# Forgetting attention: the gate bias of the scores spread over the partitions by one transfer per head and added in PSUM by VectorE, in place of a matmul by TensorE

## The reference, cut to what matters

```
c = cumsum(log_sigmoid(f_logit), axis=1)            # (heads, tokens), one value per head and token
s = q @ k.T / sqrt(dh)
s = s + c[query] - c[key]
s = where(key <= query, s, -inf)
p = softmax(s);  o = p @ v
```

## Time and profile before

| what | value |
|---|---|
| median of 3 runs | 1056.45 us (1056.3 to 1057.19) |
| the profiled execution, its own time | 1057.25 us |
| its span (first to last instruction) | 1055.4 us |
| PE busy | 1047.5 us (99%) |
| DVE busy | 750.2 us (71%) |
| ACT busy | 593.8 us (56%) |
| mean granted TensorE clock | 0.998 of full speed |

### The profile page before, as it was taken

The page is one execution under the profiler, slowest core; times in us unless marked ns, Lnnn a source line. Parts: engine busy times, 40 slices in busy tenths (PEclk is TensorE's granted clock), DMA queues, the critical chain, the costliest instruction groups (busy, mean ns, idle before and its releaser), DMA issues.

```text
span 1055.4 us, 12979 instructions
## 1 busy us (share of the span) xinstructions
PE 1047.5 (99%) x4971; PEld 875.6 (83%) x4971; DVE 750.2 (71%) x898; ACT 593.8 (56%) x794; POOL 75.5 (7%) x59
## 2 busy tenths in 40 slices
PE   9999999999999999999999999999999999999997
PEld 7888888888888888888888888888889988888886
DVE  5768778885786676467986878868778666767642
ACT  6573776764484645448754545554366657565531
POOL 1200000000000000000454600000000000000000
PEclk9999999999999999999999999999999999999999
DMA  9944999986488777555547855979975345777741
GB/s 355 399 131 172 302 298 291 303 259 197 176 276 248 241 232 233 183 207 192 160 160 226 241 172 169 285 243 334 318 246 186 118 166 208 238 244 230 247 161 40
DMA packets 94765, 239.68 MB, mean 227 GB/s; under 512 B 14785, under 2 KB 39537, under 8 KB 94577
## 3 DMA queue, kind: packets, MB, share of 16 engines
q1 hardware_dynamic: 91136, 227.32, 66.9%
q0 software_dynamic: 3136, 11.23, 2.9%
q10 hardware_dynamic: 432, 0.33, 0.1%
HBM read 218.38 MB, written 20.45 MB: 226 GB/s over the span
## 4 chain that ended last, share of the span: by engine, by line
PE 90%; DVE 4%; ACT 2%; DMA 2%; issue 2%; SPq 0%; DVEq 0%; ACTq 0%
PE ps L810 21%; PE ps L808 21%; PE ps L809 21%; PE ps L845 5%; PE ps L847 5%; PE ps L846 5%; DVE rest L1936 1%; PE ps L942 1%; PE ps L1132 1%; ACT high L1363 1%; PE ps L1248 1%; PE ps L1250 1%; PE ps L1249 1%; DMA mk_blocked<-mem_turned 1%; DMA mem_turned<-mk_blocked 1%
## 5 line engine op out<-in xcount | busy, mean ns | idle before, releaser
L1936 DVE TENSOR_TENSOR rest<-raw,high 128x2048 fp32r<-128x2048 f32 x129 | 294.3, 2297 | 78.2 <-ACT high L1363 77.7
L808 PE MATMUL ps<-high,xt_high 128*128 128x512 f32 x824 | 324.6, 394 | 0.2 <-DVE rest L1936 0.2
L810 PE MATMUL ps<-high,xt_rest 128*128 128x512 f32 x824 | 320.9, 389 | 0.0
L809 PE MATMUL ps<-rest,xt_high 128*128 128x512 f32 x824 | 320.8, 389 | 0.0
L1363 ACT ACTIVATE high<-raw 128x2048 fp32r<-128x2048 f32 x129 | 244.3, 1910 | 67.8 <-DMA raw<-in_units_dram 67.7
L810 PEld LDWEIGHTS ps<-high,xt_rest 128*128 128x128 f32 x824 | 154.7, 188 | 32.3
L808 PEld LDWEIGHTS ps<-high,xt_high 128*128 128x128 f32 x824 | 154.8, 188 | 31.8 <-DVE rest L1936 0.6
L809 PEld LDWEIGHTS ps<-rest,xt_high 128*128 128x128 f32 x824 | 154.8, 188 | 31.1
L1941 DVE SCALAR_TENSOR_TENSOR rest<-raw,wgain,high 128x512 fp32r<-128x512 f32 x176 | 119.0, 746 | 35.4 <-ACT high L1367 35.4
L1367 ACT ACTIVATE high<-raw,wgain 128x512 fp32r<-128x512 f32 x176 | 110.9, 716 | 9.1 <-DMA raw<-in_units_dram 9.0
L1623 ACT ACTIVATE act<-ps,recips 128x256 f32<-128x256 f32 x44 | 18.4, 470 | 85.0 <-PE ps L810 85.0
(11 more groups left out here) (365 smaller groups left out, 1450.7 us busy)
## 6 DMA issues: line engine op xcount, KB each, us to landing
raw<-in_units_dram SPq DMA_DIRECT2D x350, 512.0 KB, 4.7
gv_turned<-gv_blocked SPq DMA_DIRECT2D x11, 512.0 KB, 5.6
gv_t<-gv_turned SPq DMA_DIRECT2D x44, 128.0 KB, 4.1
turned<-blocked SPq DMA_DIRECT2D x22, 256.0 KB, 5.3
hid_t<-turned SPq DMA_DIRECT2D x88, 64.0 KB, 4.1
raw<-in_units_dram SPq DMA_DIRECT2D x8, 256.0 KB, 5.2
fp_turned<-fpT SPq DMA_DIRECT2D x8, 192.0 KB, 2.7
fpT<-fp_turned SPq DMA_DIRECT2D x32, 48.0 KB, 3.6
```

The costliest lines, as they stand in the source:

```text
L808: pe.matmul(out, sh, wh, start=first, stop=False)
L809: pe.matmul(out, sh, wr, start=False, stop=False)
L810: mm = pe.matmul(out, sr, wh, start=False, stop=last)
L1936: vec.tensor_tensor(rest[:, slot, c], raw[:, slot, c], high[:, slot, c].bitcast(F32), ALU.subtract).then_inc(unit_rest, 1)
```

## The change

The bias matmul of each head is taken out of PE's work, with the matrix `identr`, the cleared buffer, the rounded copy and the remainder. The eight rows of `fcum` go to a DRAM tensor once. Per head, one transfer reads that head's row from DRAM to all 128 partitions (128 x 256 float32 numbers, 128 KB written), into one of two buffers. DVE adds it to the scores in PSUM with two instructions (128 and 256 columns) before it takes the maxima. The mask matmul now opens the accumulation. SP gets the new function `spread_biases`, called last in each load: the store on load 13 of `win2`, the transfer of head h on load 31 + h.

```diff
-        fbias = place("fbias", [P, P + S], F32R, area + 62 * KB)
+        fbias = place("fbias", [P, 2, S], F32, area + 62 * KB)
...
+        fcum_dram = nc.dram_tensor("fcum_rows", (HH, S), F32, kind="Internal").ap()
+        fcum_stored, fbias_landed = sem("fcum_stored"), [sem(f"fbias_landed{n}") for n in range(2)]
...
                 turn_probabilities(u)
+                spread_biases(u)
...
+            def spread_biases(u):
+                if u == UNIT["win2"] + 13:
+                    sync.wait_ge(sem("fcum_ready"), 1)
+                    sync.dma_start(fcum_dram, fcum[0:HH, :]).then_inc(fcum_stored, 16)
+                h = u - UNIT["win2"] - 31
+                if 0 <= h < HH:
+                    if h == 0:
+                        sync.wait_ge(fcum_stored, 16)
+                    if h >= 2:
+                        sync.wait_ge(sem("fox_max"), TT * (h - 1))
+                    sync.dma_start(fbias[:, h % 2, :], fcum_dram[h].partition_broadcast(P)).then_inc(fbias_landed[h % 2], 16)
...
-                    pe.matmul(out[:, 0:P + S], identr[:, n:n + 1].to_broadcast([P, P]), fbias[:, :], start=True, stop=False)
-                    pe.matmul(diagonal, identb[:, :], causal[:, :, :], start=False, stop=False)
+                    pe.matmul(diagonal, identb[:, :], causal[:, :, :], start=True, stop=False, skip_group_check=True)
...
-                        pe.wait_ge(sem("fcum_rest"), 2)
...
-                if u == 8:
-                    act.wait_ge(sem("fcum_ready"), 1)
-                    for c0, w in ((0, P), (P, S)):
-                        act.activation(fbias[0:FROWS, c0:c0 + w], fcum[:, 0:w], ACT.Copy).then_inc(sem("fcum_high"), 1)
...
                     elif what == "i":
+                        act.wait_ge(fcum_stored, 16)
...
-                    step(vec.memset(fbias[:, :].bitcast(F32), 0.0))
...
                         src = aux(("fs", n))
+                        vec.wait_ge(fbias_landed[n % 2], 16 * (n // 2 + 1))
+                        for c0, w in ((0, P), (P, S)):
+                            step(vec.tensor_tensor(src[:, c0:c0 + w], src[:, c0:c0 + w], fbias[:, n % 2, 0:w], ALU.add))
+                        settle()
...
-                if u == 8:
-                    vec.wait_ge(sem("fcum_high"), 2)
-                    r = slice(FROWS - HH, FROWS)
-                    for c0, w in ((0, P), (P, S)):
-                        vec.tensor_tensor(fbias[r, c0:c0 + w], fcum[r, 0:w], fbias[r, c0:c0 + w].bitcast(F32), ALU.subtract)\
-                            .then_inc(sem("fcum_rest"), 1)
```

More of the change, by code:

```diff
@@ L262, in build @@
             ("recips", [P, TT * len(NORMS)], F32), ("moments", [P, TT, 12], F32),
-            ("meanvar", [P, TT, 2], F32), ("identr", [P, HH], F32R), ("eps", [P, 2 + 2 * TT], F32), ("negmax", [P, HH, 2], F32),
+            ("meanvar", [P, TT, 2], F32), ("eps", [P, 2 + 2 * TT], F32), ("negmax", [P, HH, 2], F32),
             ("expsum", [P, HH, 2], F32), ("crossref", [P, TT * HALF], F32)):
@@ L266, in build @@
             at = -(-marks[name][1] // 32) * 32
-        identr = small["identr"]
         partsum = small["eps"][:, 2:2 + 2 * TT].rearrange("p (a t) -> p a t", a=2)
@@ L1163, in fox @@
                     out = aux(("fs", n))
-                    pe.matmul(out[:, 0:P + S], identr[:, n:n + 1].to_broadcast([P, P]), fbias[:, :], start=True, stop=False)
                     diagonal = out[:, 0:P + S].rearrange("p (n c) -> p n c", n=3)[:, 0:3:2, :]
-                    pe.matmul(diagonal, identb[:, :], causal[:, :, :], start=False, stop=False)
+                    pe.matmul(diagonal, identb[:, :], causal[:, :, :], start=True, stop=False, skip_group_check=True)
                     for tt in range(TT):
                         o = out[:, 0:P] if tt == 0 else out[:, P:P + S]
-                        mm = pe.matmul(o, fqT[:, n, tt * P:(tt + 1) * P], fox_tokens(fkT, n, *range(tt + 1)), start=False, stop=(tt == TT - 1))
+                        mm = pe.matmul(o, fqT[:, n, tt * P:(tt + 1) * P], fox_tokens(fkT, n, *range(tt + 1)), start=False,
+                                       stop=(tt == TT - 1), skip_group_check=True)
                     mm.then_inc(aux_done, 1)
@@ L2305, in _ @@
             ffn("upA", "downA", "ffn1_pre", "win2")
-            vec.tensor_tensor(identr[:, :], ident[:, 0:HH], ident[:, FROWS - HH:FROWS], ALU.add).then_inc(sem("identr_ready"), 1)
             vec.wait_ge(sem("wf_high"), 1)
```

## The result

| | before | after |
|---|---|---|
| median of the executions compared | 1056.82 us (1056.3 to 1057.52, 4) | 1089.49 us (1088.95 to 1090.51, 4) |
| span of the profiled execution | 1055.4 us | 1086.8 us |
| PE busy | 1047.5 us (99%) | 1055.1 us (97%) |
| mean granted TensorE clock | 0.998 | 0.986 |

Ratio 1.0313 with a 95% interval of 1.0300 to 1.0325: the change costs 33 us. The forecast was 1068.5 us with a range of 1059.5 to 1077. The direction was right and the size was not: the loss is almost three times the 12 us of the sum, and the time lies above the range.

A forecast was written before the change was run, and what follows sets the result against it. PE, 99% busy, was taken as the bound. Adds of 5.4 us plus bias waits of 8.7 slip a DVE-ACT loop 14.1 us; less 2.0 slack, 12.1 us later: 1068.5 us, range 1059.5 to 1077.

The forecast's parts named there:

- L: Fox slots, SP's queue: time from a bias transfer's issue to its landing, taken as 2.65 us, bounds 2.0 and 5.7.
- formula: DVE's bias waits, heads 1 to 7: seven times (0.4 us store issue plus landing time), less 12.7 us available; 8.7 us.
- rival C: Fox slots: bias transfers land late, after 4 us; waits 18.1, slip 23.5, end +21.5, 1078 us; chance 0.09.
- upper bound of 5.7 us: Bias transfer in the fox slots: longest landing time allowed, that of a transfer behind much other traffic, 5.7 us.
- The loop and the slack: Fox slots: DVE and ACT form a closed loop without PE; delays add up, beyond 2.0 us of slack before `brA`.
- The split of the waits in words: DVE's bias waits by head: some 0.7 to 0.9 us for heads 1, 2, 7, about 2.5 for heads 3 and 5.
- The adds: DVE, fox slots: two adds per head cost 0.67 us, 5.4 us for eight heads, all in the loop.
- PE's saving: PE, scores of each head: removing the bias matmul saves 0.18 us, 1.4 us for eight heads, not counted in the end.
- Slots 7 to 13: Before the fox slots: removed DVE and ACT work gains nothing; the `fcum` store and the waits around it cost nothing.
- Rival A: Fox slots: transfer hidden, only adds count, needing landing below about 1.4 us or issue a slot earlier; 1059.9 us; chance 0.12.
- Rival B: Fox slots: DVE's idle time takes the adds, slip stays below 2.0 us, PE's saving shows; 1055.0 us; chance 0.09.
- Rival D: PE after stalls at `fpT` and before `brA`: clock falls, 1.7 us per fall; 1070.2 us, two falls 1071.9; chance 0.10.

The follow-up runs named there:

- SP held: Changed kernel, but SP waits after issuing each bias transfer (except head 0's) until it has landed before issuing anything else; 1074.3 us, one execution.
- before the store: Changed kernel with each bias transfer issued directly before the 192 KB store of the probabilities instead of behind it; 1073.56 us, one execution.
- 128 copies: Changed kernel with the bias rows stored 128 times in DRAM, so each transfer reads 128 distinct rows of the right bias; 1081.31 us, one execution.
- store behind the loads: Changed kernel with the 192 KB store of the probabilities issued only behind the next unit's two loads; 1087.65 us, one execution.
- distinct rows: Changed kernel, but each transfer reads 128 different weight rows instead of one row 128 times, so the bias is wrong; 1068.88 us, one execution.
- early: Changed kernel with each head's bias transfer issued right behind the load's two unit loads, ahead of all waits for probability blocks; 1061.2 us, ratio 1.0042.
- early, reads first: Changed kernel with the bias issued right behind the unit loads and SP's probability reads ahead of the other branch's transfers; 1061.37 us, ratio 1.0043.
- adds alone: Changed kernel with only two bias transfers, both on load 31; all 16 adds stay, heads 2 to 7 reuse the data; 1060.41 us, ratio 1.0034.
- adds for 3 heads: Against the adds alone kernel, only heads 0, 1 and 2 get the two adds, heads 3 to 7 no bias; 1056.62 us, ratio 0.9993.
- tenth kernel: Changed kernel with bias transfers right behind the unit loads and probability reads ahead of the other branch's transfers, `at_rest` in its old slot; 1061.37 us.
- ninth kernel: Changed kernel with the bias stored 128 times in DRAM by a 1 MB store instead of 8 KB, each transfer reading distinct rows; 1081.31 us.
- first experiment: Changed kernel with one move: each bias transfer issued right behind the two unit loads instead of last in the load; 1061.2 us, ratio 1.0042.
- seventh kernel: Changed kernel with the bias issued right behind the unit loads and the second `at_rest` moved from slot 34 to 33; 1059.06 us, ratio 1.0025.

## Why the prediction was wrong, by its own steps

The column on the clock is what the work from the start of `brA` to the next `fpT` product took beyond 5.55 us.

| kernel | L, median (us) | DVE's waits for the bias: formula, measured | slip of the loop | clock behind the stall at `brA` | time, us |
|---|---|---|---|---|---|
| changed | 5.4 | 27.6, 27.2 | 33.2 | 2.35 | 1089.49 |
| SP held | 3.6 | 14.6, 14.3 | 20.2 | 0.0 | 1074.3 |
| before the store | 3.4 | 12.0, 11.6 | 17.6 | 1.9 | 1073.56 |
| 128 copies | 2.6 | 7.9, 8.1 | 14.2 | 2.2 | 1081.31 (9.1 of them elsewhere) |
| store behind the loads | 5.0 | 23.8, 25.6 | 31.6 | 1.9 | 1087.65 |
| distinct rows | 2.3 | 7.1, 7.1 | 13.1 | 2.2 | 1068.88 |
| early | 5.3 | none, 0 | 5.3 | 0.1 | 1061.2 |
| early, reads first | 4.9 | none, 0 | 5.35 | 2.4 | 1061.37 |
| adds alone | - | none, 0 | 5.4 | 1.5 | 1060.41 |
| adds for 3 heads | - | none, 0 | 2.0 | no stall | 1056.62 |
| no bias | - | none, 0 | 0.0 | no stall | 1054.84 |

**The step that failed: L = 2.65 us**, the time from the issue of the bias transfer to its landing, called "near the low end". Measured 5.4, a term of 37.5 us over seven heads where the sum had 18.6. Waits of 27.2 us came instead of 8.7; of the 21.0 us between forecast and measurement 18.5 are this one term, and most of the rest is the fall of the clock below. Two reasons were given for the low end, that SP had stood still before and that only the 192 KB store was in front. Both describe the queue rightly, and 128 distinct rows did land in 2.3 us there; for the one row they did not hold. The loads behind the transfer were named but not weighed, and they count for some 1.9 us; that 128 partitions read one row was named (in rival C, as unknown) but had no price of its own, and it counts for 1.2 alone and is the condition of the other. The upper bound of 5.7 us was right and the value lay just under it, but the range was cut just below C's 1078, and C's L = 4 was itself too low. With the bound kept, the sum would have gone up to 7 x 6.1 - 12.7 + 5.4 - 2.0 = +33.4 us, which holds the measured +32.7.

**The loop and the slack: right.** The slip is that of adds plus waits, to 0.1 us without waits and to 0.6 to 0.8 with them. Most of the rest is an overlap that a wait takes away: without one the adds start 0.08 us before the remainder ahead of them ends (638.28 against 636.07 + 2.29), with one they start behind it, seven times, 0.6 us. The slack of 2.0 us was that of the trace. That the waits for `fpT` come out of the same delay, the tenth kernel showed. The split of the waits in words ("0.7 to 0.9 for heads 1, 2, 7", nothing said of heads 4 and 6) does not follow from the prediction's own terms, which give 0.95, 0.95 and 1.35 and twice 0.45; the sum of 8.7 does.

**The adds: right.** 0.66 us per head against 0.67, 5.3 us for eight heads against 5.4.

**PE's saving: right in size.** The kernel without any bias is 1.4 to 1.5 us faster (0.5 to 2.3 by the interval), 0.2 us per head.

**Slots 7 to 13: right** at no cost, with the condition that the ninth kernel shows.

**Rival A** is the time of the early bias: forecast 1059.9, measured 1061.2. Of its two conditions no run had the first, an L below 1.4 (the least landing measured is 2.2); the second, an earlier issue, is the first experiment. **Rival B** fell: DVE's idle time took nothing, and the adds alone cost 3.6 us, up to 1.5 of it by the clock. **Rival C** was the right mechanism, late landing, and its L of 4 too small. **Rival D** took place as well: 2.35 us behind the last stall, where 1.7 was forecast per fall. The 1.7 came from the length of the slow stretch at the start of the span, 3.35 us; behind this stall it was 5.1 us (727.17 to 732.30). (The half level at the start was read from the durations of the earlier trace rows alone; the granted clock in the profile reads 1.00 from 0 to 3 us.) That the falls behind the stalls at `fpT` cost nothing of their own is argued and not shown: without them PE would only have arrived earlier at its next wait for the same loop.

The Trainium skill ("DMA: Bandwidth & Descriptors", the section with the chain of events behind a DMA) gave an estimate of 2.3 us for 128 KB. That page of the Trainium skill fits its figures to transfers issued from GpSimd, and here SP issues them; the distinct rows landed in 2.3 us all the same, so the trace agrees there. For the one row read 128 times the traces measure 3.3 to 3.6 us with SP held and 5.4 in place, and the measurement decides.

No version tried beats the kernel before. The best that gives every head its bias is 2.7 us slower (seventh kernel, 1059.06 against 1056.33 of the kernel before beside it), and the most to be won is 1.5 us, less than the 3.4 us that the adds cost beyond the slack (5.4 - 2.0).

## What to carry to other kernels

When a transfer is wanted soon after its issue, look at its place in the issuing queue before its size: issued a few statements earlier, an equally slow transfer made DVE wait for nothing here. Price a transfer's landing at the upper row that the trace has until its own pattern (same row for all partitions, large loads right behind it) has been seen. And look for the loop that does not contain the busiest engine: there each added microsecond counts once per turn, and a saving on the busy engine is only a longer wait.

## What the runs showed of the hardware

- One DRAM row of 1 KB read to 128 partitions: medians of 3.4 and 3.6 us from issue to landing with no load ahead and none within 0.8 us behind it, 5.0 and 5.4 with 1 MB of loads 0.4 to 0.5 us behind. 128 distinct rows of the same size at the same place: 2.2 to 2.9 us from the weights and 2.2 to 3.2 us from a scratch tensor.
- While the one row was read, the core's DMA moved 64 GB/s (head 1, 2 us), with distinct rows and the same loads behind 256 GB/s; both transfers were 128 packets of 1 KB. Why a repeated row is slow, and why it is the more easily disturbed, is open.
- Issued right behind 1 MB of loads, one row and 128 rows landed alike, in 4.2 to 4.5 us (head 0 in every kernel that has the transfer).
- Ahead of `brA` the granted clock fell to the half level (matmuls of 512 columns 0.43 us apart instead of 0.23) with PE stalls of 3.0 us (adds alone), 3.85 us (tenth kernel) and 5.3 us (changed kernel), and each fall cost 1.5 to 2.4 us; with the stall of 2.0 us in the profiled execution of the first experiment it didn't fall: from the second matmul on they were 0.24 us apart.
